# A two-layer decoder trunk with 128² retrieved experts: expert lists decoded on VectorE, a ring of 14 rows, first token block finished amid the second's picks, short end groups, loops written out

## The reference, cut to what matters

```
mod = c_act @ ada_w[l] + ada_b[l]            # 6 vectors of 1024
h = rms_norm(x, norm1_g[l]) * (1 + scale1) + shift1
...                                           # two attention branches, gates, one output projection
x = x + gate1 * (merged @ w_out[l])
h2 = rms_norm(x, norm2_g[l]) * (1 + scale2) + shift2
x = x + gate2 * peer_ffn(h2, peer_wq[l], peer_subkeys[l], peer_u[l], peer_v[l])
```

## Time and profile before

| what | value |
|---|---|
| median of 3 runs (lowest, highest) | 1972.22 us (1970.61, 1974.69) |
| profiled execution: time, span | 1970.21 us, 1968.4 us |
| mean granted TensorE clock | 0.919 |
| busy: PE, DVE, ACT, POOL | 80%, 68%, 30%, 39% of the span |
| moved by DMA | 675.88 MB, mean 343 GB/s |

### The profile page before, as it was taken

How to read it: one execution, slowest core, us unless ns; L and a number is a source line. 1 busy time by engine, 2 the same in 40 slices (tenths; PEclk the granted TensorE clock), 3 DMA queues, 4 the chain that set the end, 5 groups by cost and what they waited for, 6 DMA issues and landing times.

```text
span 1968.4 us, 20982 instructions
## 1 busy us (share of the span) xinstructions
PE 1567.1 (80%) x6028; PEld 931.2 (47%) x6028; DVE 1337.9 (68%) x3094; ACT 585.1 (30%) x1322; POOL 767.3 (39%) x1108
## 2 busy tenths in 40 slices
PE   1889979887877778777777898897878777887885
PEld 0878869433333333333366788773333333333332
DVE  5878879666666666655567787876666666666554
ACT  2445544221222222221143545432222121222222
POOL 0000006555555545555200000174565556555640
PEclk8889989988899889999988999998998998888999
DMA  8754656999999999999957556589999999999994
GB/s 346 270 180 150 235 182 235 414 421 421 418 421 417 416 412 421 421 397 422 387 192 260 172 177 207 183 346 421 419 420 420 414 422 421 412 411 413 420 422 195
DMA packets 104655, 675.88 MB, mean 343 GB/s; under 512 B 12000, under 2 KB 12128, under 8 KB 32352
## 3 DMA queue, kind: packets, MB, share of 16 engines
q0 software_dynamic: 80640, 587.24, 73.2%
q1 hardware_dynamic: 23904, 87.32, 12.7%
HBM read 673.46 MB, written 1.05 MB: 343 GB/s over the span
## 4 chain that ended last, share of the span: by engine, by line
DMA 33%; PE 26%; DVE 18%; issue 10%; ACT 6%; POOL 6%; SPq 1%; DVEq 0%; ACTq 0%; POOLq 0%
PE yac L558 18%; DMA big<-pairs,big 15%; DMA late<-pairs,big 15%; PE acc L387 4%; DVE big L840 4%; ACT wsp L358 3%; DVE wsp L366 2%; PE pg L387 2%; DMA big<-ada_pairs 2%; POOL big L1162 1%; POOL late L1162 1%; POOL big L1143 1%; DVE big L916 1%; DVE late L964 1%; DVE big L913 1%
## 5 line engine op out<-in xcount | busy, mean ns | idle before, releaser
L558 PE MATMUL yac<-big 128*128 128x512 f32 x1040 | 528.3, 664 | 168.4 <-ACT big L712 160.7
L558 PE MATMUL yac<-late,big 128*128 128x512 f32 x1008 | 490.2, 641 | 97.1 <-ACT big L712 94.2
L558 PEld LDWEIGHTS yac<-big 128*128 128x128 f32 x1040 | 214.5, 212 | 477.9 <-issue 262.2
L558 PEld LDWEIGHTS yac<-late,big 128*128 128x128 f32 x1008 | 204.3, 206 | 377.1 <-issue 255.3
L1162 POOL DMA_INDIRECT big<-pairs,big x260 | 250.2, 962 | 293.0 <-PE yac L558 237.9
L387 PE MATMUL acc<-hs,wsp 128*128 128x256 f32 x2400 | 323.8, 296 | 32.2 <-DVE hs L824 30.7
L387 PEld LDWEIGHTS acc<-hs,wsp 128*128 128x128 f32 x2400 | 309.7, 201 | 43.7 <-DVE hs L824 32.3
L1162 POOL DMA_INDIRECT late<-pairs,big x252 | 237.0, 940 | 229.1 <-PE yac L558 173.5
L703 ACT ACTIVATE big<-big 128x4 f32<-128x4 f32 x128 | 26.3, 205 | 802.1 <-DVE big L964 782.9
L964 DVE CUSTOM_DVE_ANT_0 late<-late,acc 128x1024 f32<-128x1024 f32 x128 | 156.0, 1221 | 135.0 <-DMA late<-pairs,big 133.2
L1122 POOL DMA_DIRECT2D big<-ada_pairs x48 | 25.7, 535 | 567.9 <-DVE mod L840 378.8
(11 more groups left out here) (148 smaller groups left out, 1249.8 us busy)
## 6 DMA issues: line engine op xcount, KB each, us to landing
raw<-stream SPq DMA_DIRECT2D x140, 512.0 KB, 3.5
big<-ada_pairs POOLq DMA_DIRECT2D x48, 1024.0 KB, 6.8
big<-ada SPq DMA_DIRECT2D x16, 512.0 KB, 15.2
big<-pairs,big POOLq DMA_INDIRECT x260
late<-pairs,big POOLq DMA_INDIRECT x252
big<-subkeys SPq DMA_DIRECT2D x2, 1024.0 KB, 12.2
x<-xT SPq DMA_DIRECT2D x1, 1024.0 KB, 6.9
outT<-big SPq DMA_DIRECT2D x1, 1024.0 KB, 3.9
```

Of the source, the lines that this page charges most:

```text
L558: mm = pe.matmul(yac[:, 2 * t + w, :], diag(n), row(n)[:, D + w * 512:D + (w + 1) * 512], start=(n % (SLOTS // TT) == 0), stop=(n % (SLOTS ...
```

## The change

1. **Decode on DVE.** `topk_record` goes on to compute the unit's 16 expert numbers (three pairs of operations on 128x256 and three small ones) and signals `index_done`; `decode` on POOL is gone. The 16-column copy in `scores_in` is gone.
2. **Ring of 14**, eight of them in `big` (the query buffer shrinks to four column blocks, `QP`). Gathers 8 to 11 wait each for one query product (12 to 15), gather 12 for `h2_by_tokens`.
3. **Block 0 early.** ACT copies its sum once pick 127 is added (it stands after group 34), PE transposes it (`turn`) after pick 144, DVE adds (`add_half`), ACT squares, PE sums the squares (`ssq_half`) after pick 168. At the end only block 1 is left, and `Sqrt`'s table is loaded before the last sum.
4. **Short end groups**: the last four picks are groups of 2, 1 and 1.
5. **Next layer early.** SP waits for the last list instead of the layer's end, then loads `par`, the sub-keys and, as chunks are split, weights; the first three chunks of layer 2 are split and its first `mod` is made amid the last 16 picks. POOL's `ada_pairs` loads for layer 2 no longer wait for the layer's end.
6. **No hardware loops**: the two layers and the inner loops are written out.

```diff
-RING = 12
+RING = 14
-GROUPS = SLOTS // GROUP
+SHORT = [(SLOTS - 4, SLOTS - 2), (SLOTS - 2, SLOTS - 1), (SLOTS - 1, SLOTS)]
+GROUP_OF = [(n, n + GROUP) for n in range(0, SLOTS - GROUP, GROUP)] + SHORT
+GROUPS = len(GROUP_OF)
+EARLY = SLOTS // TT + 16
...
-            with sp.Fori(0, depth, 1) as L:
-
-                sp.wait_ge(ytok_taken, nth(L, 2, 2))
+            for L in range(depth):
+
+                if L:
+                    sp.wait_ge(topk_done, L * UNITS)
...
                 for n in range(SLOTS):
                     add_pick(L, n)
+                    if n == EARLY:
+                        turn(L, 0, B_YT0)
+                    if n == EARLY + 24:
+                        ssq_half(L, 0)
+                turn(L, 1, B_YT1)
+                ssq_half(L, 1)
...
+                    if g == EARLY // GROUP - 2:
+
+                        act.wait_ge(slot_done, nth(L, SLOTS, SLOTS // TT))
+                        nc_act.activation(col(B_YT0, D), yac[:, 0:2, :], ACT.Copy).then_inc(y0tok_taken, 1)
...
+                act.preload_act_table(ACT.Sqrt)
                 act.wait_ge(slot_done, nth(L, SLOTS, SLOTS))
-                nc_act.activation(col(D, D), yac[:, 2:4, :], ACT.Copy).then_inc(ytok_taken, 1)
+                nc_act.activation(col(B_YT1, D // 2), yac[:, 2, :], ACT.Copy).then_inc(ytok_taken, 1)
...
+                for p in range(2):
+                    d.mark(v.tensor_tensor(eqs[p], rec[:, 32 + 16 * p:48 + 16 * p].unsqueeze(2).to_broadcast(shape),
+                                           iota16.unsqueeze(1).to_broadcast(shape), ALU.is_equal))
+                d.join()
+                for p in range(2):
+                    d.mark(v.tensor_tensor(eqs[p], eqs[p], rec[:, 16 * p:16 * p + 16].unsqueeze(1).to_broadcast(shape),
+                                           ALU.mult))
+                d.join()
+                for p in range(2):
+                    d.mark(v.tensor_reduce(top(K_PRES + 16 * p, 16), eqs[p], AX.X, ALU.add))
...
+                            if SHORT[0][0] - GROUP == GROUP_OF[g][0]:
+                                dve_low(dve, L + 1, 0)
+                                dve_low(dve, L + 1, 1)
...
-                    if n == RING_BIG:
-
-                        pool.wait_ge(chunk_done, W + (L + 1) * SPLITS)
+                    if RING_BIG <= n < RING_BIG + W:
+
+                        pool.wait_ge(chunk_done, (L + 1) * SPLITS + n - RING_BIG + 1)
```

More of the change, by code:

```diff
@@ L562, in _ @@
             pe.wait_ge(inputs_in, 80)
-            with pe.Fori(0, depth, 1) as L:
-                ssq(nth(L, 2, 1))
+            for L in range(depth):
+                if L == 0:
+                    ssq(1)
                 for c in range(N_QA):
@@ L586, in _ @@
                         head_values(L, s - 4)
-                with pe.Fori(0, N_BR // 4, 1) as i:
+                for i in range(N_BR // 4):
                     for c in range(4):
@@ L594, in _ @@
                         product(pe, pg[:, c % 2, T:2 * T], M_BR + c, 4, 8, L, first).then_inc(chunk_done, 1)
-                with pe.Fori(0, N_OUT // 4, 1) as i:
+                for i in range(N_OUT // 4):
                     for c in range(4):
@@ L707, in pick_diag @@
                 act.wait_ge(weight_done, nth(L, GROUPS, g + 1))
-                for n in range(g * GROUP, (g + 1) * GROUP):
+                for n in range(*GROUP_OF[g]):
                     if n >= DIAGS:
@@ L718, in _ @@
             nc_act.activation(cosT[:, :], qk(1), ACT.Sin).then_inc(rope_table, 1)
-            with act.Fori(0, depth, 1) as L:
-                act.wait_ge(ytok_taken, nth(L, 2, 2))
-                for m in range(AHEAD - 1):
-                    act_high(act, L, m)
-                last_squares(L)
+            for L in range(depth):
+                if L == 0:
+                    for m in range(AHEAD):
+                        act_high(act, L, m)
+                    squares(0, KD)
                 root(nth(L, 2, 1))
-                act_high(act, L, AHEAD - 1)
                 act.wait_ge(mod_ready, nth(L, 1, 1))
@@ L759, in _ @@
                 act.wait_ge(acc_free, nth(L, EVACS, E_WQ + 2))
-                with act.Fori(0, N_BR // 4, 1) as i:
+                for i in range(N_BR // 4):
                     for c in range(4):
@@ L1049, in _ @@
                 d.clear()
-                with dve.Fori(0, N_BR // 4, 1) as i:
+                for i in range(N_BR // 4):
                     for c in range(4):
@@ L1080, in _ @@
                         for part in range(4):
[L1081 removed]
+                            topk_part(L, u, part)
                 dve.wait_ge(ada_free, nth(L, N_ADA, N_ADA))
@@ L1164, in gather @@
                         row_in[n % RING], 16)
-                decode(0)
-                for u in range(UNITS):
-                    pool.wait_ge(decode_done, L * UNITS + u + 1)
-                    for q in range(PICKS):
-                        if q == (PICKS // 2 if u else RING_BIG) and u + 1 < UNITS:
-                            decode(u + 1)
-                        gather(u * PICKS + q)
+                for n in range(SLOTS):
+                    if n % PICKS == 0:
+                        pool.wait_ge(index_done, L * UNITS + n // PICKS + 1)
+                    gather(n)
 def to_stream(w):
```

196 lines of the change are left out of this document (112 added, 84 removed).

## The result

The changed kernel takes 1949.16 us (median of 4 runs, 1947.9 to 1952.24), the kernel before 1972.38 us (4 runs beside it, 1970.61 to 1974.69): ratio 0.9884, 95% interval 0.9867 to 0.9901, so 23 us or 1.2% faster. 1935 us was forecast, in a range of 1921 to 1949. The direction was right, the gain was two thirds of the forecast one, and the time lies 0.2 us above the range's upper end, within rival A's 1946 to 1950.

What follows compares the result with a forecast made beforehand. Gathers were taken to bound two thirds of the time. From 1970.2 us, -11.3 in the stage, -6.0 - 9.5 between layers and -6.0 - 2.4 at the end made -35.2: 1935 us, range 1921 to 1949.

Steps and rivals of the forecast that it cites:

- rival A: Expert stage gives nothing, later products and holes eat the early start; only the ends pay: 1946 to 1950, chance 0.20.
- First gather: At each expert stage's start, decode on DVE takes 3.6 instead of 14.2 us: 10.6 us a layer gained.
- Stream dry: Among the query products, gathers 8 to 13 wait and DMA runs dry: 3.5 us a layer lost.
- Bytes in the stage: Three more weight loads fall into each stage, 7.4 us; next-layer loads at layer 1's end, 5.9 us.
- Holes: Inside the stages, no POOL decode and 14 rows close the DMA stream's holes: 10.4 us gained, bounds 0 and 10.4.
- Short end group: At each stage's end, a last group of one cuts PE's work from 7.13 to 1.1 us: 6.0 a layer gained.
- Copy to reciprocal: From the sums' copy to the reciprocal takes 5.4 us: 9.5 us gained after layer 1, 2.4 in layer 2.
- B: Rival: the stream never runs dry and layer 1's end loads cost nothing: 1925, or 1921 with cheaper decode; chance 0.20.
- C: Rival: POOL's gather issue becomes the bound; at 2.65 us each the time is 2016; chance 0.03.

Runs made afterwards that it cites:

- decode_pool: The changed kernel with the decode of every unit back on POOL, in the middle of a unit's gathers: 1953.01 us, ratio 0.9912 to the kernel before.
- decode_dve: The kernel before with all hardware loops written out and every unit's decode on DVE, ring of 12 and one gate kept: 1978.62 us.
- one_gate: The changed kernel, but gathers 8 to 11 all wait for the last query product: 1958.39 us.
- loads_last: The changed kernel, but the next layer's sub-keys, vectors and first three chunks' splits come only after the last pick again: 1952.60 us.
- loops_out: The kernel before with all hardware loops written out, nothing else: 1962.40 us.
- shorter_ends: The changed kernel with the last eight picks as groups of 2, 2, 1, 1, 1 and 1 instead of 4, 2, 1 and 1: 1950.06 us.
- groups_of_4: The changed kernel with the last four picks in one group again: 1956.14 us.

## Why the prediction was right or wrong

- **First gather, -10.6 a layer.** Right: -12.0 and -11.1. Nine DVE operations took 3.0 us as forecast. Its net worth with the dry stream and the three weight loads was forecast at 3.4 a layer. decode_pool shows 2 to 3 by the ratio, near the noise, and 1.2 us in all at layer 2's last dot; without gates that open one by one (decode_dve) it is worth less than nothing.
- **Stream dry, +3.5 a layer.** Right: gathers 8 to 11 within 1.2 us of the forecast, 4.4 instead of 5.1 us lost, and one_gate shows that such loss counts.
- **Bytes in the stage, +7.4 and +5.9.** About right: loads_last measures 4.8 for the 5.9, and the 2.5 us by which 144 picks of layer 1 are slower are the 2.6 of the sub-keys. No run takes the 7.4 by itself; with the late first gather of decode_pool the stages are 8.7 and 9.9 us shorter, where the dry stream and the three loads were to make 7.2.
- **Holes, -10.4: the step that failed.** "With no decode on POOL and 14 rows I take all of it back." The holes were there and were closed, the mean rate rose from 417 to 421 GB/s, and 144 picks of layer 2 still took 362.3 instead of 362.1 us. I had priced a row by the mean of 16 engines; as I read the traces, a pick is complete when its last DMA engine is, and that one was not idle in the holes. With this term at zero the forecast stage lengths are 670.5 and 663.4 us; measured are 668.4 and 664.4. By this reading the holes only kept the 15 other engines' lead short, 2.5 instead of 8.6 us at the end. The bound that I gave (0 to 10.4) held the truth, and I took the wrong end.
- **Short end group, -6.0 a layer: the term that was mis-sized.** "PE then needs 7.13 us for eight picks" was a misreading of x16: four records a pick, so four picks. The 7.13 us were one group of four. With a last group of one, 1.76 us were to be left behind the last weight, not 1.1; and the picks end at 1932.1, 4.7 us after the last diagonal (1927.46), since the last eight picks take 14.1 us and PE can start on the first of them only at 1918.09. Measured -3.2 and -3.0.
- **Copy to reciprocal, -9.5 and -2.4.** Right: -8.9 and -1.8; the sum of squares has 16 records, not four matmuls' worth, 2.19 us. In layer 1 the number is better than its working: loops_out shows that the 5.54 us of idle DVE go with the loops, but that they ran beside ACT and PE. What made the stretch long was ACT's late start, PE's sum at a low clock and a late reciprocal (2.9, 2.8 and 1.4 us). By the Trainium skill (Runtime: NRT & Kernel Launch, Instruction fetch mechanics) a branch taken outside the current pages stalls for a fetch. The idle times of 5.54 us on DVE and 1.84 on ACT, gone in loops_out, agree with it; no row shows the fetch itself.
- **A reading.** The prediction has the DMA at 9 in slices 8 to 17; the row shows 8 to 20. Nothing in the sum used it.
- **The sum.** The holes (10.4) and the short group (5.8) make 16.2 of error; the other terms gave 2 us more than forecast. 1935 + 14.2 = 1949.2.
- **The rivals.** A's time came, and more of its mechanism than I had given it: "the stage gives nothing" was nearly so, 3.9 us of the 23.1 by which the gathers start earlier, and decode_dve shows the early start eaten by later products. But the slow windows inside the stage did not remain, and the ends gave 16.9 instead of A's 23.9, so the total agrees with A partly by luck. B and C did not show; POOL's issues inside the stage took 0.94 us and waited for picks to be added.

Shown by runs: that DVE's fetches delay the rows, by about 1 us for 8 KB, and that POOL's and ACT's do not; that the higher mean rate brought no faster dots; the worth of the gates; the clock's part in shorter_ends; ACT's wait. Only argued: that there is one late DMA engine and that DVE's fetches lie on it, from the sixteenth of the rate that is left at the end and from single late dots; the trace names no DMA engine. Open: why a packet of 0.32 us costs about 1 us.

## What to carry to other kernels

When a stage is bound by DMA, look at its end in short windows before counting on its mean rate: if a sixteenth of the rate runs on after the rest has stopped, one DMA engine may set the pace, and closing holes in the mean may buy nothing, as here. The pace of the dots over many picks tells it better than the mean rate. Let the early gathers through one by one as their buffers come free, and keep the engine whose instruction fetches delay the rows (here DVE) short of instructions. When the last groups are made small, check three things at once: how many records a pick has on PE, whether the clock survives the gaps, and which engine's program has another wait ahead of the small group.

## What the hardware showed that I had not expected

- 1024 empty instructions a layer on DVE cost 8.3 us a layer in a DMA-bound stage, though DVE had slack; the same number on POOL or ACT cost under 2 us a layer by the ratios, and nothing in the pace of 144 dots. By the Trainium skill (Runtime: NRT & Kernel Launch, Instruction fetch mechanics) such fetches are "mostly hidden" and come in blocks of 16 KiB. The runs differ: q8 here has 16 KB packets (48 with 0.79 MB), q14 8 KB ones, and DVE's are not hidden: hidden from the engine, they are paid by the rows.
- PE's clock fell towards the 1.2 GHz level in the last group of some runs: behind an idle time of 2.72 us the same 16 records took 8.83 us in groups_of_4 (granted clock 0.66), while behind 2.75 us of idle time they took 7.13 us in the earlier trace rows. The idle time just ahead does not decide it alone.
